# Taking the unread products out of TensorE's waits in the routing of a mixture-of-experts kernel

## The reference

```
logits = (ht @ w_router).astype(jnp.float32) + b_router.astype(jnp.float32)
top_v, top_i = lax.top_k(logits, TOP_K)
probs = jax.nn.softmax(top_v, axis=-1)
gates = jnp.sum(jax.nn.one_hot(top_i, N_EXPERTS, dtype=jnp.float32) * probs[..., None], axis=1)
for e in range(N_EXPERTS):
    a = jax.nn.silu(ht @ w_gate[e]) * (ht @ w_up[e])
    out = out + gates[:, e:e + 1] * (a @ w_down[e]).astype(jnp.float32)
```

## Time and profile before

| what | before |
|---|---|
| median of three runs | 1729.98 us |
| the profiled execution | 1730.03 us |
| its span, first to last instruction | 1728.3 us |
| around the span (the difference) | 1.7 us |
| TensorE busy | 1719.8 us of the span |
| VectorE busy | 1382.6 us |
| ScalarE busy | 1102.5 us |
| mean granted TensorE clock | 1.000 |

### The profile page before, as it was taken

One profiled execution on the slowest core, in us unless ns is written; L12 is line 12 of the kernel. 1 busy time (PEld: TensorE's weight loads), 2 busy tenths in 40 slices (PEclk: granted clock), 3 DMA queues, 4 the chain that ended last, 5 costly groups with the idle time before them and its releaser, 6 DMA issues.

```text
span 1728.3 us, 22641 instructions
## 1 busy us (share of the span) xinstructions
PE 1719.8 (100%) x8320; PEld 1436.2 (83%) x8320; DVE 1382.6 (80%) x1146; ACT 1102.5 (64%) x980; POOL 112.9 (7%) x114
## 2 busy tenths in 40 slices
PE   9999999999999999999999999999999999999998
PEld 8888888888888888888888888888888888888887
DVE  7875587555578755889888889889888898898898
ACT  4446564444344466647777777777777777777775
POOL 0021000000000200017100000000000000000100
PEclk9999999999999999999999999999999999999999
DMA  8663366554455524659999999999999999999995
GB/s 293 231 206 117 122 244 219 195 186 130 171 170 197 171 90 146 219 220 331 411 361 411 372 369 403 375 370 401 345 409 381 356 410 373 367 401 375 374 413 199
DMA packets 219848, 498.41 MB, mean 288 GB/s; under 512 B 8296, under 2 KB 13168, under 8 KB 219632
## 3 DMA queue, kind: packets, MB, share of 16 engines
q1 hardware_dynamic: 216096, 483.44, 76.0%
q0 software_dynamic: 3696, 14.18, 2.2%
HBM read 491.80 MB, written 7.88 MB: 289 GB/s over the span
## 4 chain that ended last, share of the span: by engine, by line
PE 96%; ACT 1%; DVE 1%; DMA 0%; issue 0%; POOL 0%; SPq 0%; DVEq 0%; POOLq 0%
PE ps L764 30%; PE ps L766 30%; PE ps L765 30%; PE ps L773 4%; PE ps L769 3%; ACT sb_w L1447 0%; DVE sb_wlo L395 0%; DMA sb_ringa<-in_w_in_dram 0%; ACT sb_whi L380 0%; DVE sb_w L1721 0%; ACT sb_ahi L1504 0%; DVE sb_z L1831 0%; ACT L1447 0%; DVE sb_wlo L424 0%; ACT sb_z L1497 0%
## 5 line engine op out<-in xcount | busy, mean ns | idle before, releaser
L424 DVE TENSOR_TENSOR sb_wlo<-sb_z,sb_whi 128x2048 fp32r<-128x2048 f32 x334 | 756.5, 2289 | 95.4 <-ACT sb_whi L418 94.6
L418 ACT ACTIVATE sb_whi<-sb_z 128x2048 fp32r<-128x2048 f32 x333 | 634.9, 1927 | 169.0 <-PE ps L766 162.8
L764 PE MATMUL ps<-sb_whi,sb_hhi 128*128 128x512 f32 (+2 forms) x1752 | 684.3, 391 | 0.3
L766 PE MATMUL ps<-sb_wlo,sb_hhi 128*128 128x512 f32 (+2 forms) x1752 | 675.9, 386 | 0.0
L765 PE MATMUL ps<-sb_whi,sb_hlo 128*128 128x512 f32 (+2 forms) x1752 | 675.7, 386 | 0.0
L766 PEld LDWEIGHTS ps<-sb_wlo,sb_hhi 128*128 128x128 f32 x1752 | 329.0, 188 | 66.8
L764 PEld LDWEIGHTS ps<-sb_whi,sb_hhi 128*128 128x128 f32 x1752 | 329.3, 188 | 66.3 <-issue 3.2
L765 PEld LDWEIGHTS ps<-sb_whi,sb_hlo 128*128 128x128 f32 x1752 | 329.4, 188 | 63.0
L764 PE MATMUL ps<-sb_whi,sb_ahi 128*128 128x512 f32 x560 | 219.1, 391 | 0.0
L766 PE MATMUL ps<-sb_wlo,sb_ahi 128*128 128x512 f32 x560 | 218.0, 389 | 0.0
L765 PE MATMUL ps<-sb_whi,sb_alo 128*128 128x512 f32 x560 | 218.0, 389 | 0.0
(11 more groups left out here) (272 smaller groups left out, 967.3 us busy)
## 6 DMA issues: line engine op xcount, KB each, us to landing
sb_z<-in_moe_w_gate_dram SPq DMA_DIRECT2D x112, 1024.0 KB, 7.2
sb_z<-in_moe_w_up_dram SPq DMA_DIRECT2D x112, 1024.0 KB, 7.7
sb_z<-in_moe_w_down_dram SPq DMA_DIRECT2D x112, 1024.0 KB, 7.3
sb_ringa<-in_w_in_dram SPq DMA_DIRECT2D x43, 1024.0 KB, 5.1
sb_z<-in_w_in_dram SPq DMA_DIRECT2D x24, 1024.0 KB, 5.2
sb_z<-in_ffn_w_up_dram SPq DMA_DIRECT2D x10, 1024.0 KB, 5.0
sb_z<-in_ffn_w_gate_dram SPq DMA_DIRECT2D x10, 1024.0 KB, 5.0
sb_z<-in_ffn_w_down_dram SPq DMA_DIRECT2D x10, 1024.0 KB, 5.0
```

Source lines behind the costliest of these rows:

```text
L418: nc.scalar.activation(e_lane(s)[0], ringb[:, s % RING_B, :], ACT.Copy).then_inc(hi_done, 1)
L424: nc.vector.tensor_tensor(lo, ringb[:, s % RING_B, :], hi.bitcast(F32), ALU.subtract).then_inc(split, 1)
L764: nc.tensor.matmul(out, lh, rh, start=start, stop=False)
L766: return nc.tensor.matmul(out, lh, rl, start=False, stop=stop)
```

## The change

The helper `fill` and its five calls go, and so does the wait for the weight tile ahead of the first of them. All else stays as it was, in the same order, on all engines.

```diff
-            def fill(n):
-
-                slot = e_lane(0)[0]
-                for _ in range(n):
-                    mm(ps[:, 0, 0:S], slot[:, 0:P], slot[:, 0:S])
...
                     else:
                         turn_rest()
-                        wait_lo(pe, 1, "B", 0)
-                        fill(14)
                     for k in range(KH * h, KH * h + KH):
                         if h == 1 and k % 2 == 0:
-                            if k > KH:
-                                fill(2)
                             pe.wait_ge(ht_lo, 4 * (3 * layer + 2) + k // 2 + 1)
...
                 m.then_inc(router_mm, 1)
-                fill(4)
                 pe.wait_ge(logit_sb, 1)
...
                 m.then_inc(lg_mm, 1)
 
-                fill(19)
                 pe.wait_ge(sel_ok, 1)
...
                 mm(ps[:, 4, 0:NE], ones, rt[:, 1, :], start=False).then_inc(cnt_mm, 1)
-                fill(5)
```

## The result

The changed kernel takes 1732.85 us (median of 19 runs, 1732.24 to 1734.58), against 1729.98 us of before in as many runs (1729.42 to 1730.89). The ratio is 1.0017 with a 95% interval from 1.0011 to 1.0023. It is slower by 2.9 us; the prediction had 1732.8. The profiled execution took 1733.21 us, 3.2 us more than that of before, of which the span has 1731.5.

The account below looks back on a forecast made before the run. TensorE, busy 1719.8 of 1728.3 us, was taken to bound the kernel. Gather +2.6, counts +0.3 and the five's gap -0.1 gave +2.8 us on 1730.03, so 1732.8 us; range 1729.6 to 1734.4.

Parts of the forecast that it names:

- The products cost nothing by themselves: Routing: the unread products lie beside VectorE's chain, which paces the stretch; removing all 44 is by itself worth 0.1 us.
- The 0.1 us won by the five: Before the gather: without the five products it starts 0.05 instead of 0.15 us after VectorE's matrix, -0.1 us.
- The clock falls: Emptied routing: TensorE drops to 1.2 GHz between 766 and 770 us, total +2.8 us; chance 0.62.
- the case that the prediction kept for its upper bound: Routing: the clock falls already in the first idle piece, before 763.4 us, and the whole gather runs slow; +4.4 us.
- The gather, +2.6 us: Gather at 1.2 GHz for 5.2 us: 23 of 32 instructions slow, 6.2 us instead of 3.65.
- The counts, +0.3 us: Eight count matmuls at 1.2 GHz: the first four end 0.46 us later, delaying the gather by 0.3 us.
- No slack behind it: After the gather: TensorE has no slack, so all the gather's loss, +2.6 us, reaches the end.
- The rival of the clock that holds: Routing: the clock stays up, leaving only the -0.1 us, 1729.9 us; chance 0.30.
- The absorbed loss: After the routing: the clock falls but converting engines getting ahead win the loss back, 1730.1 us; chance 0.04.
- The slow return to 1735: Gather and expert products: the clock falls and stays slow some 10 us, +5 us and 0.3, 1735.2 us; chance 0.04.

Follow-up runs that it names:

- the second profile: The changed kernel, all 44 unread products out against the kernel before, profiled in one more execution: 1734.22 us.
- the 19 alone: Kernel before with the 14, 2, 4 and 5 unread products out, only the 19 before the counts kept: median 1732.19 us; profiled executions 1730.06 and 1731.94 us.
- the early 20: Kernel before with the 19 and 5 unread products out, the 14, 2 and 4 kept: median 1732.74 us, ratio 1.0014.
- the late 24: Kernel before with the 14, 2 and 4 unread products out, the 19 and 5 kept: median 1732.26 us, ratio 1.0013.
- only the 5: Kernel before with the 14, 2, 4 and 19 unread products out, the 5 between counts and gather kept: median 1733.38 us, ratio 1.0019.

## Why the prediction was right, step by step

- **The products cost nothing by themselves.** Held: each step up to the counts starts within 0.01 us of where it did, once the 0.11 us is allowed for. That is so because the clock fell late there. In the second profile, with the fall in the router's second half, the counts start 0.81 us late.
- **The 0.1 us won by the five.** Wrong: the gather follows VectorE's matrix by 0.15 us with them and without, at full clock and at half. The term should have been 0.
- **The clock falls.** Held in both profiles of the change, and all 19 runs are over 1732 us. I put the fall at 766 to 770 us; it came at 766.5 and, in the second profile, at 764.1, near the case that the prediction kept for its upper bound. That the granted clock reads 1.00 beside the 421 ns was taken from a row of 1.04 to 4.30 us; the stretch of 5.30 to 6.20 us reads 1.00 as well.
- **The gather, +2.6 us.** Measured +2.88. The slow phase under steady work was 5.2 us in the sum and 776.8 - 770.75 = 6.0 in the profile; about 26 of 32 instructions ran slow, not 23. The mechanism and the price of one (0.23 against 0.114, measured 0.22) were right and the length was somewhat small. The sum let the slow phase begin its 5.2 us at the gather; in the profile it lasted 10.3 us in all, 4.2 of them ahead of the gather. It was read from one event at the start of one trace. In the profile of the change itself the same constant-input products near the start take 275 ns in the median and 298 at most, where before had four of them at 421, so that length varies from one execution to the next.
- **The counts, +0.3 us.** Measured +0.38, with VectorE's wait of 0.41 us on TensorE as its row. In the second profile all that lies ahead of the gather comes to +1.18 us.
- **No slack behind it.** Held: 954.3 us from the first expert product to the end in both.

2.6 + 0.3 - 0.1 = 2.8 came out near the 3.18 of the profiled pair and very near the 2.87 of the medians. The nearness to the median is partly luck: in the profiled pair the terms for the gather and the counts were each too small and the 0.1 us was not won, and single runs of the change spread over 2.3 us, 1732.24 to 1734.58, by where the slow phase begins and ends.

The rival of the clock that holds is refuted for the change. It is half true of milder edits: with the 5 or the 14 out, 6 or 7 of 11 executions stay below 1731 us. The absorbed loss is refuted by the 954.3 us. The slow return to 1735 is not seen in the change; its ingredients, an early fall and a late rise, gave 1734.2 once, and the slowest of the 19 runs, 1734.58, was not profiled.

The rule of the Trainium skill's page "TensorE: Matmul & The Clock Gate", Part 1, that activity releases the throttle and idling lets it back, agrees with the traces: 0.50 of the granted clock behind the idle piece. The run with 8 columns adds that a fall needs no idle piece over 0.32 us. That recorded clock events can mislead was seen only at the start of the program; in the routing the column and the durations agree in each profile, 421 ns where the gather ran at 0.50 and 275 where it ran at 1.00.

What stays open is why the same kernel falls in some executions and not in others. The traces of the 19 alone show two executions whose lists and idle pieces are alike up to 763.5 us, one at 1.00 and one that falls. What makes the difference was not found in the profile.

## What to carry to other kernels

Where TensorE waits for a chain of small steps and has dense work behind it, the price of leaving it empty is not the wait but the work behind: here 3.6 us of gather became 6.4. Unread products are free only while the clock is up and they end before what they wait beside; with a group too few, the rest can find themselves at half clock and become the path. Their width matters too: products of 8 columns took about as long as those of 256 and did not keep the clock up. Judge such an edit by many executions and by the share that falls, since a single profile, as the first one of the 19 alone, can show none of it.

## What the runs showed of the hardware that was not expected

- A fall can come while TensorE is already at work again: 0.50 from 771.3 to 774.7 us, under a gather that ran without a break from 770.56.
- An idle piece of 1.9 us with the other waits filled goes with times over 1731 us in 5 of 11 executions; one of 2.8 us, together with the empty wait before the gather, in 11 of 11.
- The clock fell at 765.3 us under a list with no idle piece over 0.32 us in the routing, where the 44 products had 8 columns in place of 256.
- The slow phases seen lasted 3.4 us (the 5 out), 6.8 us (19 alone, the early 20, and the late 24), 10.2 us (only the 5), 10.3 and 13.7 us (the change), and 13.7 us (8 columns).
- At 1.2 GHz products of 8 and of 256 columns on 128 columns of weights cost nearly the same, 0.21 and 0.22 us each.
